# High and low words of a two-block transformer's hidden activations, interleaved word by word in SBUF

## What is computed

```python
def swiglu_ffn(x, w_gu, w_down):
    g, u = jnp.split(x @ w_gu, 2, axis=-1)      # 1024 -> 2 x 2816
    return (jax.nn.silu(g) * u) @ w_down        # 2816 -> 1024
...
    z = val * jax.nn.sigmoid(gate)              # state-space mixer, 1024 wide
    return (z @ w_out).astype(x.dtype)
...
    return (o @ w_o).astype(x.dtype)            # stick-breaking attention
...
    mixed = jax.nn.sigmoid(g_a) * (att @ w_att_branch) + jax.nn.sigmoid(g_m) * (hm @ w_m_branch)
    x = x + mixed @ w_out
    u = jax.nn.relu(rmsnorm(x, norm_ffn) @ w_ff1)
    return x + (u * u) @ w_ff2                  # 1024 -> 4096 -> 1024
```

## Time and profile before

| | us |
|---|---|
| median of 2 runs | 1345.89 (1345.70 to 1346.08) |
| the profiled execution, own time | 1345.26 |
| its span, first to last instruction | 1343.5 |

### The profile page before, as it was taken

How to read it: one execution, slowest core, us unless ns; L and a number is a source line. 1 busy time by engine, 2 the same in 40 slices (tenths; PEclk the granted TensorE clock), 3 DMA queues, 4 the chain that set the end, 5 groups by cost and what they waited for, 6 DMA issues and landing times.

```text
span 1343.5 us, 25805 instructions
## 1 busy us (share of the span) xinstructions
PE 1314.9 (98%) x10699; PEld 1246.5 (93%) x10699; DVE 944.1 (70%) x1277; ACT 676.0 (50%) x838; POOL 58.9 (4%) x31
## 2 busy tenths in 40 slices
PE   5899999999999999999999999999999999999999
PEld 4699999988999999998989999998898999999988
DVE  8966976657865986657897787775457867877542
ACT  5774643334765643344666545444445554544332
POOL 6910000000000000000000000000000000000000
PEclk9999999999999999999999999999999999999999
DMA  8676586675443576666444446567664535556661
GB/s 157 159 187 185 133 218 186 188 189 182 145 145 97 155 210 185 188 190 175 149 141 143 155 160 217 189 182 194 188 188 126 157 122 194 189 187 187 188 188 63
DMA packets 342808, 227.80 MB, mean 170 GB/s; under 512 B 22616, under 2 KB 337792, under 8 KB 342592
## 3 DMA queue, kind: packets, MB, share of 16 engines
q1 hardware_dynamic: 341200, 226.33, 58.6%
q10 hardware_dynamic: 1520, 0.20, 0.1%
HBM read 224.40 MB, written 1.05 MB: 168 GB/s over the span
## 4 chain that ended last, share of the span: by engine, by line
PE 86%; DVE 7%; ACT 4%; issue 1%; POOL 1%; DMA 0%; SPq 0%; DVEq 0%; ACTq 0%; POOLq 0%
PE PS L419 20%; PE PS L420 20%; PE PS L421 20%; PE PS L429 12%; PE PS L430 6%; DVE w_lo L400 2%; ACT w_hi L395 1%; PE PS L1340 1%; DVE xn L1134 1%; DVE xn L1129 1%; DMA c_rows<-in_ssm_c_re_dram 0%; PE PS L1742 0%; PE PS L2409 0%; PE PS L1324 0%; DVE raw_lo L1089 0%
## 5 line engine op out<-in xcount | busy, mean ns | idle before, releaser
L400 DVE TENSOR_TENSOR w_lo<-raw,w_hi 128x2048 fp32r<-128x2048 f32 x207 | 473.5, 2290 | 144.1 <-ACT w_hi L395 143.0
L419 PE MATMUL PS<-x_hi,w_hi 128*128 128x256 f32 x1792 | 504.0, 281 | 0.9 <-DVE w_lo L400 0.5
L420 PE MATMUL PS<-x_lo,w_hi 128*128 128x256 f32 x1792 | 503.7, 281 | 0.0
L421 PE MATMUL PS<-x_hi,w_lo 128*128 128x256 f32 x1792 | 503.3, 281 | 0.0
L395 ACT ACTIVATE w_hi<-raw 128x2048 fp32r<-128x2048 f32 x207 | 396.4, 1915 | 203.3 <-PE PS L430 139.1
L419 PEld LDWEIGHTS PS<-x_hi,w_hi 128*128 128x128 f32 x1792 | 338.3, 189 | 6.0 <-issue 2.9
L420 PEld LDWEIGHTS PS<-x_lo,w_hi 128*128 128x128 f32 x1792 | 336.6, 188 | 0.1
L421 PEld LDWEIGHTS PS<-x_hi,w_lo 128*128 128x128 f32 x1792 | 336.7, 188 | 0.0
L429 PE MATMUL PS<-hid_both,w_hi 128*128 128x512 f32 x756 | 264.8, 394 | 0.0
L430 PE MATMUL PS<-hid_both,w_lo 128*128 128x256 f32 x756 | 211.8, 280 | 0.0
L429 PEld LDWEIGHTS PS<-hid_both,w_hi 128*128 128x128 f32 x756 | 142.1, 188 | 31.4
(11 more groups left out here) (394 smaller groups left out, 1481.5 us busy)
## 6 DMA issues: line engine op xcount, KB each, us to landing
raw<-in_w_ff_dram SPq DMA_DIRECT2D x128, 512.0 KB, 4.6
raw<-in_ffn_w_gu_dram SPq DMA_DIRECT2D x88, 512.0 KB, 5.1
raw<-in_w_in_dram SPq DMA_DIRECT2D x68, 512.0 KB, 4.7
raw<-in_sb_w_qkv_dram SPq DMA_DIRECT2D x24, 512.0 KB, 4.5
raw<-in_ffn_w_down_dram SPq DMA_DIRECT2D x20, 512.0 KB, 4.9
raw<-in_ssm_w_glu_dram SPq DMA_DIRECT2D x16, 512.0 KB, 5.5
raw<-in_w_out_dram SPq DMA_DIRECT2D x16, 512.0 KB, 4.5
raw<-in_ssm_w_out_dram SPq DMA_DIRECT2D x8, 512.0 KB, 4.6
```

What stands on the lines that cost most here:

```text
L400: nc.vector.tensor_tensor(w_lo[s][:, :], raw[s][:, :], w_hi[s][:, :].bitcast(F32), ALU.subtract).then_inc(lo_done, 1)
L419: nc.tensor.matmul(dst, lhs_hi, r_hi, start=start, stop=False, skip_group_check=True)
L420: nc.tensor.matmul(dst, lhs_hi, r_lo, start=False, stop=False, skip_group_check=True)
L421: return nc.tensor.matmul(dst, lhs_lo, r_hi, start=False, stop=stop, skip_group_check=True)
```

## The change

The k-tile of `hid_both` is stored as 256 pairs of a high word and its low word; a view with the old order of dimensions is laid over it, so `hid_hi` and `hid_lo` become views with a step of 2 words (8 bytes), for PE's reads and for VectorE's writes and reads. In `two` the 512 columns keep their order, the high words first and then the low ones, so the PSUM bank is filled as before; the moving pattern has two dimensions, 2 x 256 with steps of 1 and 2 words. The number, order, waits and sizes of all instructions stay.

```diff
@@ -280,7 +280,7 @@
         x_lo = sb("x_lo", [P, KT, T], "xl", 0, F32R)
-        hid_both = sb("hid_both", [P, 32, 2, T], "hh", 0, F32R)
+        hid_both = sb("hid_both", [P, 32, T, 2], "hh", 0, F32R).rearrange("p k t i -> p k i t")
         hid_hi, hid_lo = hid_both[:, :, 0, :], hid_both[:, :, 1, :]
@@ -426,7 +426,8 @@
         def two(bank, lhs_hi, lhs_lo, both, start, stop):
 
-            nc.tensor.matmul(PS[:, bank, :], lhs_hi, both.rearrange("p i t -> p (i t)"), start=start, stop=False, skip_group_check=True)
+            nc.tensor.matmul(PS[:, bank, :].rearrange("p (i t) -> p i t", i=2), lhs_hi, both, start=start, stop=False,
+                             skip_group_check=True)
             return nc.tensor.matmul(PS[:, bank, 0:T], lhs_lo, both[:, 0, :], start=False, stop=stop, skip_group_check=True)
```

## The result

The changed kernel takes 1757.21 us (median of 2 runs, 1756.84 to 1757.58) against 1345.89: 1.305 times as long, 95% interval 1.3032 to 1.3076. The span of its profiled execution is 1755.8 us, 412.3 more than before. Lines behind 429 have moved by one: line 430 of before is 431.

A forecast was written before the change was run, and what follows sets the result against it. The prediction took PE's stream of matmuls to bound the kernel (PE busy 98%). 1345.3 us of profiled execution plus nothing for reads and writes, with the runs' median 0.6 us above, gave 1346 us; range 1325 to 1390.

The forecast's parts named there:

- the two ends of the moving reads: PE's stepped reads of `hid_both`: either no cost or a halved rate, 367 us more; no cost was taken.
- the 64-byte row: Profile row of 32 PE weight loads, 128 words 64 bytes apart: 0.110 us each, 0.86 ns a word, read as no loss.
- the lower end: PE's moving reads of `hid_both` cost nothing more with the step: 1340 to 1352 us, chance 0.60.
- The ACT row: Profile row: ACT takes 632 ns for 512 contiguous words, 1133 for words 256 bytes apart; kept the upper end possible.
- the upper end: PE's moving reads of `hid_both` fall to one word per 0.84 ns: 367 us more, 1713 us, chance 0.18.
- the excess of 16 and 10 ns: Time per 512- and 256-column float32r matmul beyond 0.418 ns a column plus 164 ns, which plain rows don't have.
- the 1713 that I had for the case: Forecast time in us if PE's moving reads of `hid_both` ran at half rate: 1346 + 367, chance 0.18.
- Doubles: Rival: moving reads and weight loads meet twice as often in SBUF, +34 us, 1380; 1352 to 1385 had chance 0.15.
- shrinks: Rival: a luckier address pattern removes excess, 1334 us if only line 429 gains, 1312 if all; chance 0.07.
- The writes at no cost: DVE's stepped casts and subtractions into `hid_both` would keep their times, 294 and 427, 426 and 692 ns.
- DVE's cover: DVE's chunk work, 3.43 or 4.10 us, at worst 5.43, stays under the 5.7 us PE needs for a chunk.

The follow-up runs named there:

- the plain float32 pair: Matmuls on `hid_both` in plain float32, against the kernel before: with the changed layout 2591.93 us, with the old layout 2517.12 us.
- the adjacent plain kernel: The kernel before with the matmuls on `hid_both` in plain float32, old layout, adjacent words: 2517.12 us, ratio 1.8695.
- the two kernels with stepped weights: The kernel before with weights of the matmuls on `hid_both` read at a step of 64 bytes (1460.04 us) or 8 bytes (1351.37 us).
- the 128-byte runs: The kernel before with PE reading aligned runs of 16 words that start 128 bytes apart: 1359.94 us, ratio 1.0103.
- 16 over 64 bytes: The kernel before with PE reading every fourth word (step of 16 bytes), 1772.17 us, or every sixteenth (64 bytes), 1722.69 us.

## Why the prediction was wrong

**The step that failed** is the choice between the two ends of the moving reads: "I take no cost, since the 64-byte row is the nearest on PE." Three things were wrong with taking that row. It is of weight loads, and at 0.86 ns a word they run at half the rate of float32r moving rows (0.45), so whatever a step takes away from the faster rate can't be seen in it. It is of another kind of load: given to the loads of these matmuls, a step of 64 bytes cost 1.8 ns a word, not 0.86. And even at its own word, that loads go to a new place every 0.86 ns, it tells of one word per place; that a place gives two words in the same time was my addition. The runs show that it doesn't: 128 groups with one word each take 110 ns (220 for 256 columns at 64 bytes), 128 groups with two words each take 228. None of the rows has float32r rows read with a step, so they left both ends open, and my 0.60 for the lower end leaned on the loads of line 1658. The ACT row, 1.8 times the time for one word per place, pointed to the upper end.

**The bounds.** The upper end had the right mechanism, the rate halves and all of it is on the path, but each term was too small. Of the 512-column matmuls I had 198 ns more, by distances it is 221 (452 - 231); of the 256-column ones 97 or 98, it is 110. The halved rate isn't 0.84 ns a column but 0.88, since the excess of 16 and 10 ns that I had found did not go away but grew to about 22 and 13 (452 - 430 and 228 - 215): the step costs the slower path something too, 21 and 10 ns a record in the plain float32 pair. 756 x 0.221 + 756 x 0.110 + 1,476 x 0.110 = 167 + 83 + 162 = 412 us against my 367. The time is 44 us above the 1713 that I had for the case. The 378 and 592 ns that I had read as one plain matmul are one of its two records; the sum used them as a rate alone, so this did not change it.

**Its mechanism in my words**, that a read gives 8 adjacent bytes and two words 8 bytes apart need two reads, was wrong all the same: pairs of adjacent words are as slow. The piece is an aligned group of 16 bytes, and it goes at the full rate only if four of its words are read.

**The Trainium skill's rule** (SBUF — State Buffer, Specifications (TRN2)), lines of 16 bytes that need at least two hits each, has the right size of the piece. The weight loads of these matmuls agree with it: two words of a group gave loads of 192 and 195 ns, close to the 188 of adjacent words, one word gave 0.30 to 0.32 us. The loads of line 1658 don't, at one word per place and 0.110 us from start to start. Float32r and bfloat16 moving rows don't either: two hits a line gave 228 ns for 256 columns, four gave 118 or 114. Here the measurement decides: four hits were enough, two and three were not.

**The excess.** "Doubles" and "shrinks" were both beside the point as whole cases. That plain rows have no excess was no finding, since two durations always lie on a line; the distances of the adjacent plain kernel, 216 and 429 ns, do give 0.84 ns a column for both sizes. That stands for adjacent words only.

**What held.** The bound: a kernel as long as its stream of matmuls, each nanosecond of which counts; the growth by counts and distances closes to 1 us. The 2,988 matmuls on `hid_both`, with no instruction added. The writes at no cost, and DVE's cover. `x_hi`'s matmuls unchanged. The sign to look for, a larger chain share of lines 429 and 431 and longer idle times of DVE and ACT.

**What stays open.** Why one word of a group is no slower than two on the moving path: 220 ns for 256 columns at 64 bytes means a new group every 0.86 ns, 228 at 8 bytes one every 1.8 ns. A single limit on groups per time fits the two kernels with stepped weights, but not the moving rows; it looks as if a group that isn't read whole is fetched anew for each word, which is only argued. The small costs of the 128-byte runs, of 16 over 64 bytes and of three and one words are unexplained, and so are the loads of line 1658 at 0.110 us each.

## What to carry to other kernels

Moving rows that stream at the full rate (float32r, bfloat16) should be read in whole, aligned groups of 16 bytes of 4-byte words, or at least four words out of each group; interleave high and low words by four, not by one. Where a cost has two far ends, don't take the row that is nearest on the engine but one of the same kind of read at the same rate, and where there is none, as here, leave both ends open: reads at half rate can't show what the full rate needs. A price in the stream is read from the distance of starts; the modelled end in the durations added 25 ns here to each 512-column matmul (640 - 394 = 246 against 221).

## What the hardware showed that I had not expected

- Of a group of 16 bytes, three words are no better than one: 232 to 237 ns for 256 columns in runs split three and one, against 118 for four.
- The rate changes within one instruction, group by group: 164 to 170 ns for a row with half of its words in whole groups.
- A larger step need not cost more: 434 ns for 512 columns at 64 bytes, 461 at 16 (over fewer different words).
- A plain float32 matmul is two records of 0.84 ns a column, so it costs 3.7 times a float32r one: 2 x 429 against 231 ns for 512 columns.
- bfloat16 weight loads at a step of 4 bytes take 97 and 98 ns, float32r ones 188; the matmuls gained little by it, 226 and 114 ns against 231 and 118.
